# Zero-padded queries and unnormalised mixing in the differential attention of a two-block kernel

## What is computed

```python
q = rms_norm(q, q_norm[l])                 # per head and map, width d = 64
k = rms_norm(k, k_norm[l])
s = einsum("bhmqd,bhmkd->bhmqk", q, k) * scale + bias       # m: the two maps
p = softmax(where(causal, s, -1e30))
a = p[:, :, 0] - lam * p[:, :, 1]
o = einsum("bhqk,bhkd->bhqd", a, v)
o = rms_norm(o, subln_g) * (1.0 - lam_init)                  # eps 1e-6
```

## Time and profile before

| | |
|---|---|
| runs | 1729.07, 1729.44, 1729.72 us; median 1729.44 us |
| profiled execution: span from first to last instruction | 1727.7 us (its own time isn't given apart) |
| PE busy | 1700.7 us, 98% of the span |
| DVE, ACT, POOL busy | 68%, 53%, 17% |
| granted clock of PE | 1.000 in the mean |
| the mixer's scores, layer 0 and layer 1 | from 994.6 and from 1479.3 us |

### The profile page before, as it was taken

The page is one execution under the profiler, slowest core; times in us unless marked ns, Lnnn a source line. Parts: engine busy times, 40 slices in busy tenths (PEclk is TensorE's granted clock), DMA queues, the critical chain, the costliest instruction groups (busy, mean ns, idle before and its releaser), DMA issues.

```text
span 1727.7 us, 25216 instructions
## 1 busy us (share of the span) xinstructions
PE 1700.7 (98%) x9721; PEld 1458.1 (84%) x9721; DVE 1175.8 (68%) x1565; ACT 922.0 (53%) x1269; POOL 297.4 (17%) x162
## 2 busy tenths in 40 slices
PE   8999999999999999999999999999999999999999
PEld 8768888899888788878888978888888889878887
DVE  5887666778476875577666876666666667856665
ACT  4664444546674544465446566444554456664443
POOL 6003000675250130010000830000000006500000
PEclk9999999999999999999999999999999999999999
DMA  9425655556405575536564523665465554435652
GB/s 283 151 86 187 226 194 177 168 154 198 142 1 168 168 237 193 179 127 209 193 194 146 196 98 123 218 192 187 156 209 184 191 187 160 141 98 195 194 194 98
DMA packets 204268, 293.83 MB, mean 170 GB/s; under 512 B 6474, under 2 KB 169776, under 8 KB 204192
## 3 DMA queue, kind: packets, MB, share of 16 engines
q1 hardware_dynamic: 201072, 285.56, 50.6%
q0 software_dynamic: 2688, 6.47, 1.4%
q10 hardware_dynamic: 432, 0.75, 0.1%
HBM read 291.71 MB, written 1.05 MB: 169 GB/s over the span
## 4 chain that ended last, share of the span: by engine, by line
PE 89%; DVE 5%; ACT 4%; issue 1%; POOL 1%; DMA 0%; SPq 0%; ACTq 0%; DVEq 0%; POOLq 0%
PE acc L2078 30%; PE pg L2078 14%; PE pg L2152 13%; PE pg L2156 12%; PE pg L2155 6%; PE pg L2153 6%; PE acc L2616 1%; ACT w_hi L852 1%; PE pg L2603 1%; PE pg L2718 1%; ACT arena L1054 1%; PE pg L2198 1%; POOL w_lo L752 1%; ACT op L867 1%; DVE op L1421 1%
## 5 line engine op out<-in xcount | busy, mean ns | idle before, releaser
L1383 DVE TENSOR_TENSOR w_lo<-w_raw,w_hi 128x2048 fp32r<-128x2048 f32 x231 | 539.7, 2338 | 162.7 <-ACT w_hi L852 162.6
L852 ACT CAST w_hi<-w_raw 128x2048 fp32r<-128x2048 f32 x269 | 513.0, 1908 | 66.4 <-PE pg L2078 28.3
L2078 PE MATMUL acc<-w_hi,op 128*128 128x512 f32 x1600 | 517.5, 393 | 1.7 <-DVE op L2008 1.6
L2152 PE MATMUL pg<-op,w_hi 128*128 128x512 f32 x960 | 382.3, 398 | 7.0 <-DVE op L1413 1.9
L2156 PE MATMUL pg<-op,w_hi 128*128 128x512 f32 x960 | 379.7, 395 | 0.0
L2078 PEld LDWEIGHTS acc<-w_hi,op 128*128 128x128 f32 x1600 | 300.3, 188 | 66.9 <-issue 7.4
L2078 PE MATMUL acc<-w_lo,op 128*128 128x512 f32 x800 | 311.5, 389 | 0.0
L752 POOL TENSOR_TENSOR w_lo<-w_raw,w_hi 128x2048 fp32r<-128x2048 f32 x38 | 175.1, 4615 | 682.6 <-DVE w_lo L1383 630.2
L2155 PE MATMUL pg<-op,w_lo 128*128 128x256 f32 x960 | 267.6, 279 | 0.0
L2153 PE MATMUL pg<-op,w_lo 128*128 128x256 f32 x960 | 266.4, 277 | 0.0
L2078 PE MATMUL pg<-op,w_hi 128*128 128x256 f32 x1184 | 222.9, 287 | 2.9 <-DVE op L1421 1.2
(11 more groups left out here) (342 smaller groups left out, 1704.3 us busy)
## 6 DMA issues: line engine op xcount, KB each, us to landing
w_raw<-in_mlp_w SPq DMA_DIRECT2D x64, 1024.0 KB, 5.3
w_raw<-in_ffn_w_gate SPq DMA_DIRECT2D x44, 1024.0 KB, 5.3
w_raw<-in_ffn_w_up SPq DMA_DIRECT2D x44, 1024.0 KB, 5.3
w_raw<-in_ffn_w_down SPq DMA_DIRECT2D x44, 1024.0 KB, 4.8
w_raw<-in_ssm_w_in SPq DMA_DIRECT2D x24, 1024.0 KB, 5.3
w_raw<-in_w_in SPq DMA_DIRECT2D x20, 1024.0 KB, 5.1
w_raw<-in_attn_w_in SPq DMA_DIRECT2D x8, 1024.0 KB, 10.1
w_raw<-in_ssm_w_out SPq DMA_DIRECT2D x8, 1024.0 KB, 4.9
```

What stands on the lines that cost most here:

```text
L852: act.copy(w_hi[:, u % RING, :], w_raw[:, u % RING, :]).then_inc(hi_ready, 1)
L1383: dve.tensor_tensor(w_lo[:, s, :], w_raw[:, s, :], w_hi[:, s, :].bitcast(F32), ALU.subtract) \
L2078: ins = pe.matmul(psum, l, r, start=first and i == 0, stop=last and i == 2)
L2152: pe.matmul(bank, hi, joined, start=k == 0, stop=False)
```

## The change

Queries are evacuated into a buffer of two planes, one for each map, whose other 64 partitions hold zeros; the keys stay as they are. A score product then runs over all 128 partitions. The two maps are mixed as `e0 + r * e1` with `r = -lambda * s0 / s1`, where e0 and e1 are exponentials and s0 and s1 their row sums, so the row carries a factor s0 too many. The norm behind it takes the factor out, if its epsilon is multiplied by s0 squared: `seps` holds that, for each token tile and head, and the root of the output norm is taken in four pieces, each with its own bias. The squares of the convolution move out of the `arena` into two buffers of the MLPs.

```diff
-        Q2 = cv(DH, T)
+        Q2 = cv(2, DH, T)
...
-        osq = cv(4, T)
...
-        r2 = cv(8, 2)
+        r2 = cv(DH, TT)
+        seps = cv(DH, TT)
...
+        osq = (act_pair, h_pair)
...
+        def padded_queries(n, m):
+
+            c = 2 * ((n - 4) // 2)
+            return Q2[m * HD:(m + 1) * HD, m, c:c + 2, :].rearrange("p c t -> p (c t)")
...
             def o2_root(l, a):
 
-                act.activation(odev[:, a, :], odev[:, a, :], ACT.Sqrt, bias=lnb[:, 1:2], scale=1.0 / P) \
-                    .then_inc(osq_std, 1)
+                act.wait_ge(seps_ready, DH * l + 2 * a + 2)
+                for k in range(2 * TT):
+                    ins = act.activation(odev[:, a, k:k + 1], odev[:, a, k:k + 1], ACT.Sqrt,
+                                         bias=seps[:, 2 * a + k // TT, k % TT:k % TT + 1], scale=1.0 / P)
+                ins.then_inc(osq_std, 1)
...
-                    act.activation(head_pair(n), pg[:, n % 4, :], ACT.Identity, scale=pcol[:, gc:gc + 1])
+                    if n % 2:
+                        act.activation(head_pair(n), pg[:, n % 4, :], ACT.Identity, scale=pcol[:, gc:gc + 1])
+                    else:
+                        for m in range(2):
+                            rows = slice(m * HD, (m + 1) * HD)
+                            act.activation(padded_queries(n, m), pg[rows, n % 4, :], ACT.Identity,
+                                           scale=pcol[rows, gc:gc + 1])
...
                 dve.memset(uu[:, :, 0:CK - 1], 0.0)
+                for m in range(2):
+                    dve.memset(Q2[(1 - m) * HD:(2 - m) * HD, m, :, :], 0.0)
...
                     dve.wait_ge(ex2_done, 8 * l + 2 * h + 2)
-                    link(dve.reciprocal(r2[:, 2 * h:2 * h + 2, :], s2[:, 2 * h:2 * h + 2, :]))
+                    link(dve.reciprocal(r2[:, h, :], s2[:, 2 * h + 1, :]))
+                    link(dve.scalar_tensor_tensor(out=r2[:, h, :], in0=r2[:, h, :], scalar=nlam[:, l:l + 1],
+                                                  in1=s2[:, 2 * h, :], op0=ALU.mult, op1=ALU.mult))
+                    dve.scalar_tensor_tensor(out=seps[:, h, :], in0=s2[:, 2 * h, :], scalar=EPS2, in1=s2[:, 2 * h, :],
+                                             op0=ALU.mult, op1=ALU.mult).then_inc(seps_ready, 1)
...
-                    mixed = pg[:, 3, 0:384] if h == DH - 1 else acc[:, 2, 0:384]
                     for a, z, qt in ((0, P, 0), (P, 384, 1)):
-                        link.mark(dve.tensor_scalar(mixed[:, a:z], prob2[:, b1, a:z], r2[:, 2 * h + 1, qt:qt + 1],
-                                                    nlam[:, l:l + 1], ALU.mult, ALU.mult))
-                    for a, z, qt in ((0, P, 0), (P, 384, 1)):
-                        link.all_but(1 - qt)
-                        ins = dve.scalar_tensor_tensor(out=pmix[:, k % 2, a:z], in0=prob2[:, b0, a:z],
-                                                       scalar=r2[:, 2 * h, qt:qt + 1], in1=mixed[:, a:z],
+                        ins = dve.scalar_tensor_tensor(out=pmix[:, k % 2, a:z], in0=prob2[:, b1, a:z],
+                                                       scalar=r2[:, h, qt:qt + 1], in1=prob2[:, b0, a:z],
                                                        op0=ALU.mult, op1=ALU.add)
...
-                    pe.matmul(pg[:, s % 2, 0:P], Q2[p0:p0 + HD, h, 0:P], K2[p0:p0 + HD, h, 0:P], start=True,
-                              stop=True)
-                    pe.matmul(pg[:, s % 2, P:384], Q2[p0:p0 + HD, h, P:T], K2[p0:p0 + HD, h, :], start=True,
-                              stop=True).then_inc(sc2_done, 1)
+                    pe.matmul(pg[:, s % 2, 0:P], Q2[:, m, h, 0:P], K2[:, h, 0:P], start=True, stop=True)
+                    pe.matmul(pg[:, s % 2, P:384], Q2[:, m, h, P:T], K2[:, h, :], start=True, stop=True) \
+                        .then_inc(sc2_done, 1)
```

More of the change, by code:

```diff
@@ L558, in two_blocks @@
         o2_norm = sem("o2_norm")
+        seps_ready = sem("seps_ready")
         oT_done = sem("oT_done")
@@ L580, in head_pair @@
             c = 2 * ((n - 4) // 2)
-            return (K2 if n % 2 else Q2)[:, c:c + 2, :].rearrange("p c t -> p (c t)")
+            return K2[:, c:c + 2, :].rearrange("p c t -> p (c t)")
+        def padded_queries(n, m):
+            c = 2 * ((n - 4) // 2)
+            return Q2[m * HD:(m + 1) * HD, m, c:c + 2, :].rearrange("p c t -> p (c t)")
         class Link:
@@ L1297, in conv_square @@
                 def conv_square(c):
-                    act.activation(osq[:, c:c + 2, :], cacc[:, c:c + 2, :], ACT.Square).then_inc(csq, 1)
+                    act.activation(osq[c // 2], cacc[:, c:c + 2, :], ACT.Square).then_inc(csq, 1)
                 u, o = U_MIX[l], U_MIX_OUT[l]
@@ L1350, in _ @@
                         k = COL["conv_norm"] + 4 * l + c
-                        ins = act.activation(c32[:, c, :], osq[:, c, :], ACT.Silu, scale=pcol[:, k:k + 1])
+                        ins = act.activation(c32[:, c, :], osq[c // 2][:, c % 2, :], ACT.Silu, scale=pcol[:, k:k + 1])
                     link(ins)
@@ L2000, in conv_scale @@
                     for c in range(2):
-                        dve.tensor_tensor(osq[:, c, :], cacc[:, c, :], acc[:, 3, 0:T], ALU.mult).then_inc(cnorm, 1)
-                    dve.tensor_tensor(osq[:, 2:4, :], cacc[:, 2:4, :],
+                        dve.tensor_tensor(osq[0][:, c, :], cacc[:, c, :], acc[:, 3, 0:T], ALU.mult).then_inc(cnorm, 1)
+                    dve.tensor_tensor(osq[1], cacc[:, 2:4, :],
                                       acc[:, 3, 0:T].unsqueeze(1).broadcast_to([P, 2, T]), ALU.mult) \
@@ L2684, in score2 @@
                 def score2(s):
-                    h, p0 = s // 2, (s % 2) * HD
+                    h, m = s // 2, s % 2
                     if s < 2:
@@ L2726, in conv_sums @@
                         for c in (c0, c0 + 1):
-                            ins = pe.matmul(acc[:, t, 0:1], osq[:, c, t * P:(t + 1) * P], ones_m,
+                            ins = pe.matmul(acc[:, t, 0:1], osq[c // 2][:, c % 2, t * P:(t + 1) * P], ones_m,
                                             start=c == 0, stop=c == 3)
```

## The result

| | before | changed |
|---|---|---|
| median of six runs each, side by side | 1729.78 us | 1734.89 us |
| lowest and highest | 1729.07, 1729.97 | 1734.06, 1735.70 |
| ratio, with its 95% interval | | 1.003 [1.002, 1.0039] |
| profiled execution: span, granted clock | 1727.7 us, 1.000 | 1732.0 us, 0.997 |

What follows compares the result with a forecast made beforehand. PE, busy nearly all the time, was taken as the bound, with DVE's score step 7 also setting the stage's end. Step 7 0.44 us late in each of two layers, other parts covered, gave +0.9 us: 1730.3 us, range 1728.5 to 1734.2.

Steps and rivals of the forecast that it cites:

- Full-row scores: PE's score products: each saves the whole 0.4 us of going to 64 rows and back, 3.2 us per layer.
- The third rival: PE's score products: 128-row scores pay the same switch as 64-row ones; 1731.0 us, chance 0.05.
- The mixing's saving: DVE's mix_head: 0.5 us instead of 0.98 before the combining, 0.48 us saved per head.
- the block: First head: DVE's two-SBUF-input operation waits 3.3 us for POOL's piece; step 3 1.70 us late, step 7 0.44.
- The first rival: First head on DVE: operations pass POOL, or its piece lies elsewhere; 2.5 us per layer gained, 1724.4 us, chance 0.12.
- The memsets: DVE, around the split ending at 582.40 + 2.29: two memsets, 1.8 us, hidden by 0.51 and 3.06 us.
- The clock: Second rival: PE's wait before the second column sums lowers its clock; 1.7 us per layer, 1733.8 us, chance 0.16.

Runs made afterwards that it cites:

- early head: Changed kernel with the first mix_head of each layer moved in front of the key norm and the four taps: 1725.68 us, ratio 0.9979.
- ratio with one tensor: Changed kernel with each head's ratio from two one-column, one-tensor operations, and seps worked out behind the combining pair: 1734.30 us, ratio 1.0026.
- the run with the wait filled: Changed kernel with 13 products with zeros in PE's queue ahead of the second column sums: 1731.13 us, ratio 1.0008.
- mixing alone: Kernel before with only the unnormalised mixing, its ratio, seps and four-piece root; 64-row products, no memsets: 1733.00 us, ratio 1.0018.
- scores alone: Kernel before with zero-padded queries, full-row scores, memsets, halved evacuation and moved squares; old mixing and root: 1728.21 us, ratio 0.9994.
- the early head and the wait filled: Changed kernel with the first mix_head earlier, memsets moved to layer 0's mixer, two zero products before the second column sums: 1724.67 us, ratio 0.997.

## Why the prediction was wrong

The forecast was 1730.3 us and no measurable change; 1734.89 came, over the end of the range. Point by point:

- **Full-row scores: right.** In the chain of the changed kernel a pair of 128 columns costs 0.22 us (once 0.33, behind sums for the norms) instead of 0.42:

```profile
995.14 0.22 PE pg L2710 x2
```

Alone they brought 1.67 us in the layer at full clock. The third rival, that they pay the same switch, is out.
- **The mixing's saving and the block: right in size and place.** 3.22 us against 3.3, step 3 1.68 late against 1.70, step 7 0.43 against 0.44; alone +0.79 against 0.76. The first rival, that the block doesn't hold here, is out. The Trainium skill, page "SBUF — State Buffer", section "SBUF: two separate sides", gave the rule for the block. The early head and the ratio with one tensor agree with it: 0.22 us without POOL's piece, and 3.26 us for the next operation with two SBUF tensors.
- **The memsets: the cover was wrong.** The step took the 0.51 us of idle and the 3.06 us between the split's end and PE's product at 587.75 as cover. But that product waits for L1507, which stands on DVE behind the split: from its end, 585.33 plus 0.69, to 587.75 there is only 1.73 us, less than the split's delay of 2.03. It cost some 0.46 us instead of nothing.
- **The clock: the step that failed.** The text gave PE's wait its right length (3.2 us; 3.05 came), left the clock out of the sum, and named it as a rival with 0.16, deciding "only if the lower clock reaches past 1029, since PE isn't the bound before". PE is a bound before: ACT's silu waits for DVE, and DVE for PE's spread, which stands behind the column sums, a head's output products and three transposes. The trace before showed it, in a row that I did not read:

```profile
1026.87 0.75 DVE L2001 TENSOR_TENSOR arena<-arena,acc 128x256 f32<-128x256 f32 x2 [0.80 <-PE acc L2735]
```

Its first half ends at 1027.3, and silu starts at 1027.41: PE had 0.1 us to spare there, not 2 us as up to 1029. At 1.2 GHz these products cost 1.02 us in layer 0 and 1.95 in layer 1. The rival's price of 3.5 us was near these 3.0 by luck: it was for the output products, which were not slowed at all (0.47 us for the first in layer 0, at 1030.88, as before the change), and its pace was that of rows whose clock figure reads full. So the lower clock was over before the place that the rival's condition names, the output products (from 1028.96 before, from 1030.88 now), and it still decided. The rival's cause came, a lower clock behind PE's wait; its chance was too low and its condition wrong. The text also had it that the trace before holds no wait like this one and that 1.07 us is the longest. That leaves out the start, where PE waited for the input, and behind which the slow products at 10.91 stand:

```profile
6.42 3.65 PE L2198 MATMUL pg<-ident,X 128*128 128x128 f32 x16 [6.42 <-DMA X<-in_x]
```

The sum at full clock, 0.46 + 0.44 + 0.45 = 1.35 us, against 0.9 forecast, would have been no measurable change, and the run with the wait filled shows it: 1.27 us over the kernel before. With 3.0 us for the clock it is the 4.3 of the profile. The median difference of 5.1 us is 0.8 larger. The other executions' clocks are no higher (0.995 to 0.997), and with the wait filled the 0.8 us is gone, so I take it for the clock too; in which layers is not known, since one execution was profiled.

## What to carry to other kernels

A faster stage on the busiest engine can turn into a wait further down, and on PE a wait can cost more than its length: price what stands behind it at the lower clock, and look for the next engine's wait for those products, however short, before calling them uncritical. Where an operation gets a second SBUF input, look at what POOL runs at that time; moving the operation by a few places in its queue was worth 3 us per layer at full clock (from +0.44 to -2.52), and PE's remaining wait can be filled with products that nobody reads. Cover for an added operation counts up to the first consumer of anything that stands behind it in its queue.

## What the runs showed of the hardware that I had not expected

- The clock fell behind short waits too, and not each time: at 0.45 us in one layer and not in the other of the same execution (early head), at 0.75 and 1.3 us in one layer each (mixing alone, scores alone), at 3.05 us in both. In the kernel before, a wait of 1.07 us at 515 was followed by full clock (1.00 from 514 to 520). With the waits filled, the profiled clock was 1.000 in both kernels tried. What decides between equal waits stays open.
- A clock that falls in some executions goes with a wider spread: 1726.83 us (clock 0.999) to 1731.47 (0.996) with the scores alone, 1724.33 to 1725.43 (1.000 and 0.999) with the early head and the wait filled.
- A DVE operation with a single SBUF tensor was held up by POOL's memset (1.12 us instead of 0.41). The Trainium skill, page "SBUF — State Buffer", section "Who interferes with whom", says that TENSOR_SCALAR can run in a mode that takes both port pairs and then contends with POOL. The row fits that, though no run shows the mode; the 128x1 operations of the same kind passed POOL's piece in 0.45 us for two.
